# Modulation rows of a two-block transformer: running sums on VectorE and one TensorE product in place of sixteen column-tiled products

## The reference, cut to what matters

```python
lam = exp(sum(lp[0] * lp[1])) - exp(sum(lp[2] * lp[3])) + lam_init
a = softmax(sc, axis=-1)                       # D head: two score maps
attn = a[:, :, 0] - lam * a[:, :, 1]
out = rmsnorm(attn @ v, subln_g) * (1.0 - lam_init)

c_act = silu(c)                                # (1, 2048)
mod = (c_act @ ada_w[l] + ada_b[l])[:, None, :]    # (2048, 12288), 100 MB
sh1, sc1, g1, sh2, sc2, g2 = split(mod, 6, axis=-1)
```

## Time and profile before

| | us |
|---|---|
| median of 3 runs | 2505.77 |
| lowest and highest run | 2504.7 to 2508.65 |
| span of the profiled execution (first to last instruction) | 2501.1 |
| TensorE busy | 2349.9 |
| VectorE, ScalarE, GpSimd busy | 847.8, 855.6, 899.7 |

### The profile page before, as it was taken

One profiled execution on the slowest core, in us unless ns is written; L12 is line 12 of the kernel. 1 busy time (PEld: TensorE's weight loads), 2 busy tenths in 40 slices (PEclk: granted clock), 3 DMA queues, 4 the chain that ended last, 5 costly groups with the idle time before them and its releaser, 6 DMA issues.

```text
span 2501.1 us, 30365 instructions
## 1 busy us (share of the span) xinstructions
PE 2349.9 (94%) x12117; PEld 1533.1 (61%) x12117; DVE 847.8 (34%) x1377; ACT 855.6 (34%) x1583; POOL 899.7 (36%) x395
## 2 busy tenths in 40 slices
PE   7999999999999998999899997999999999999997
PEld 5667777876677787778687776444444444444442
DVE  4132643122335447255443743111122211222213
ACT  4334444443344443453323643111111222111211
POOL 5465655865556567884344362000000000000000
PEclk9999999999999999999999998999999999999999
DMA  8666666576666562441222336999999999999996
GB/s 323 253 269 269 269 260 244 194 311 254 243 262 273 227 263 98 168 169 70 77 92 101 136 121 286 385 428 428 427 428 429 429 428 429 428 429 429 428 428 273
DMA packets 60518, 716.56 MB, mean 286 GB/s; under 512 B 10992, under 2 KB 11600, under 8 KB 17152
## 3 DMA queue, kind: packets, MB, share of 16 engines
q1 hardware_dynamic: 58512, 712.25, 69.6%
q10 hardware_dynamic: 1904, 2.86, 0.3%
HBM read 710.85 MB, written 4.24 MB: 286 GB/s over the span
## 4 chain that ended last, share of the span: by engine, by line
issue 39%; PE 17%; DVE 3%; ACT 1%; DMA 1%; DVEq 0%; POOLq 0%; POOL 0%; ACTq 0%
PE bank L373 5%; PE bank L427 2%; PE bank L383 2%; PE bank L437 1%; PE bank L508 1%; PE bank L514 1%; PE bank L611 1%; DMA weight_ring<-in_w_in_dram 1%; PE bank L512 1%; PE bank L476 0%; PE bank L477 0%; ACT w_hi_parts L2447 0%; PE bank L473 0%; PE bank L466 0%; PE bank L359 0%
## 5 line engine op out<-in xcount | busy, mean ns | idle before, releaser
L2135 POOL TENSOR_TENSOR weight_ring_parts<-weight_ring,w_hi_parts 128x1024 fp32r<-128x1024 f32 (+2 forms) x368 | 872.0, 2392 | 602.6 <-ACT w_hi_parts L2447 601.4
L2447 ACT ACTIVATE w_hi_parts<-weight_ring 128x1024 fp32r<-128x1024 f32 (+2 forms) x368 | 376.4, 1041 | 449.5 <-PE bank L2222 219.2
L1480 POOL TENSOR_TENSOR rms_out<-rms_in,minus_half 128x2 f32<-128x2 f32 x2 | 1.4, 697 | 967.8 <-DVE rms_in L1821 955.8
L1563 PE MATMUL bank<-weight_ring,qk_t 128*64 128x512 f32 x1024 | 224.5, 593 | 12.3 <-DMA weight_ring<-in_expert_w_up_dram 12.3
L2211 PE MATMUL bank<-w_hi_parts,h_t_parts 128*128 128x512 f32 (+1 forms) x768 | 212.9, 401 | 2.0 <-ACT w_hi_parts L2447 2.0
L2211 PE MATMUL bank<-w_hi_parts,x_res_parts 128*128 128x512 f32 (+1 forms) x768 | 198.4, 382 | 0.0
L2222 PE MATMUL bank<-weight_ring_parts,h_t_parts 128*128 128x512 f32 (+1 forms) x768 | 193.3, 380 | 0.0
L1563 PEld LDWEIGHTS bank<-weight_ring,qk_t 128*64 128x64 f32 x1024 | 77.2, 137 | 156.6 <-issue 156.6
L2211 PEld LDWEIGHTS bank<-w_hi_parts,h_t_parts 128*128 128x128 f32 x768 | 132.5, 190 | 48.8 <-issue 18.9
L2211 PEld LDWEIGHTS bank<-w_hi_parts,x_res_parts 128*128 128x128 f32 x768 | 140.5, 189 | 29.6
L2222 PEld LDWEIGHTS bank<-weight_ring_parts,h_t_parts 128*128 128x128 f32 x768 | 139.8, 188 | 28.5
(11 more groups left out here) (465 smaller groups left out, 3570.8 us busy)
## 6 DMA issues: line engine op xcount, KB each, us to landing
weight_ring<-in_w_in_dram SPq DMA_DIRECT2D x64, 2048.0 KB, 8.0
weight_ring<-in_ada_w_dram SPq DMA_DIRECT2D x48, 2048.0 KB, 11.8
weight_ring<-in_expert_w_gate_dram SPq DMA_DIRECT2D x32, 2048.0 KB, 27.0
weight_ring<-in_expert_w_up_dram SPq DMA_DIRECT2D x32, 2048.0 KB, 18.3
weight_ring<-in_expert_w_down_dram SPq DMA_DIRECT2D x32, 2048.0 KB, 24.1
weight_ring<-in_w_out_dram SPq DMA_DIRECT2D x24, 2048.0 KB, 8.7
proj<-in_expert_w_gate_dram SPq DMA_DIRECT2D x16, 2048.0 KB, 26.5
proj<-in_expert_w_down_dram SPq DMA_DIRECT2D x16, 2048.0 KB, 21.9
```

Source lines behind the costliest of these rows:

```text
L1563: last = mm(bank[side][s, :], m.xg[:, 8 * j + k, s], weights(hu + e, 8)[:, k, :], start=j == 0 and k == 0, stop=j == 1 and k == 7)
L2135: nc.gpsimd.tensor_tensor(weights(split, True), weights(split, False), rounded(split).bitcast(f32), ALU.subtract)\
L2447: A_(rounded(split), weights(split, False), ACT.Copy).then_inc(w_hi_ready, 1)
```

## The change

The sixteen products of a modulation row leave TensorE. VectorE forms a running sum over the 16 blocks: each weight block, times its column of `c` (a scalar per partition), plus the sum so far, which stands in a PSUM bank that is free at the time (bank 5 in units 0 to 5, then one of the projection banks); the last one writes the sum to SBUF (`ada_sums`, the space of the repeated column). TensorE folds the 128 partitions with one product, whose weights are one column of -0.5, and `add_row` becomes one instruction that multiplies with -2 and adds the bias. The sums are put between VectorE's tasks by a table: after which step how many of the 16 are to be done; where there is no table, all 16 stand at the unit's start, and "end" is behind the unit's tasks.

In the D heads the first map is no longer scaled by its reciprocal: the second map is weighted with the ratio of the two factors, and the common factor is put into the squares (ScalarE's scale) and into the root.

```diff
+MODS = 16
+MOD_AT = {4: {("mla_rope", 0, 0): 4, "end": 16}, 5: {"begin": 6, ("soft", "M0", 0): 10, ...
+          8: {("diff", "D1", 0): 4, ("soft", "D2", 0): 6, ("soft", "D2", 1): 12, "end": 16},
...
             for s in range(12):
+                ws, mods = [], [(("a", l, s, j), 2 + j, ("ada", l * 24 + 2 * s + j + 1)) for j in (0, 1)]
                 for j in range(1 if s == NARROW else 2):
                     n += 1
-                    keys.append((("w", l, s, j), n % 2, ("piece", ...)))
-                for j in (0, 1):
-                    keys.append((("a", l, s, j), 2 + j, ("ada", l * 24 + 2 * s + j + 1)))
+                    ws.append((("w", l, s, j), n % 2, ("piece", ...)))
+                keys += ws + mods if s == 0 else ws[:1] + mods + ws[1:]
...
         def ada(l, p):
...
-            for j in (0, 1):
...
+            pe.wait_ge(ada_used, 24 * l + 2 * p + 2)
+            nc.tensor.matmul(psTD[0:1, :], half[:, 0:1], ada_sum, start=True, stop=True).then_inc(row_summed, 1)
...
                 link(V.reciprocal(rec[:, :, :], den[:, :, :]))
-                link(V.tensor_scalar(rec[:, 1, :], rec[:, 1, :], lam[:, 1:2], None, ALU.mult))
-                for t in range(TT):
-                    last = V.tensor_scalar(pbuf[:, 0, t, :], pbuf[:, 0, t, :], rec[:, 0, t:t + 1], None, ALU.mult)
-                link(last)
+                link(V.scalar_tensor_tensor(rec[:, 1, :], rec[:, 1, :], lam[:, 1:2], den[:, 0, :], ALU.mult, ALU.mult))
...
                 dve.wait_ge(rms_ready, rr.next())
+                rec = STATS[buffer_of(arg)][5]
+                link(V.tensor_tensor(rec[:, 0, :], rec[:, 0, :], rms[:, 6:8], ALU.mult))
...
+        def mods(l, p, to):
+
+            acc = psO[:, :] if p < 6 else bank[2 * ((sums(p) + 1) % 2)][:, :]
+            while mod_at.k < to:
+                k = mod_at.k
...
+                if k == 0 and p >= 6:
+                    dve.wait_ge(pj_copied, 16 * l + sums(p))
+                if k % 8 == 0:
+                    dve.wait_ge(w_in[2 + k // 8], HALVES.loaded["a", l, p, k // 8])
+                w = ring[:, 2 + k // 8, k % 8 * U:(k % 8 + 1) * U]
+                if k == 0:
+                    ins = V.tensor_scalar(acc, w, ccol[:, k:k + 1], None, ALU.mult)
+                else:
+                    ins = V.scalar_tensor_tensor(acc if k < MODS - 1 else ada_sum, w, ccol[:, k:k + 1], acc, ALU.mult, ALU.add)
...
         def add_row(l, p):
...
-            link(V.tensor_tensor(ada_row[:, :], psTD[0:1, :], ada_b[:, :], ALU.add))
...
+            V.scalar_tensor_tensor(ada_row[:, :], psTD[0:1, :], -2.0, ada_b[:, :], ALU.mult, ALU.add).then_inc(td_copied, 1)
...
+            dve.wait_ge(setup_a, 1)
+            mod_at.k = 0
+            mods(l, 0, MODS)
             if l == 0:
...
                 if early:
                     task(l, p + 1, *early[0])
+                if p:
+                    mods(l, p, MODS)
                 add_row(l, p)
```

More of the change, by code:

```diff
@@ L2252, in ada @@
             if l + p == 0:
-                pe.wait_ge(cb_ready, 1)
+                pe.wait_ge(half_ready, 1)
             pe.wait_ge(td_copied, td.now())
-            for j in (0, 1):
[L2256 to L2262, removed]
+            pe.wait_ge(ada_used, 24 * l + 2 * p + 2)
+            nc.tensor.matmul(psTD[0:1, :], half[:, 0:1], ada_sum, start=True, stop=True).then_inc(row_summed, 1)
             td.next()
@@ L2764, in task @@
                 copy(QK[:, 11:13, :], psTD[:, :])
+                after(l, u, kind, arg, 0)
                 copy(QK[:, 15, :], psTD[:, 0:S])
@@ L2794, in task @@
                     last.then_inc(m_ready, 1)
+                    after(l, u, kind, arg, i)
             elif kind == "diff":
@@ L2813, in task @@
                     g = PROJ[:, t, DG + h * P:DG + (h + 1) * P]
[L2814 removed]
+                    last = V.scalar_tensor_tensor(g, psO[:, t * P:(t + 1) * P], rec[:, 0, t:t + 1], g, ALU.mult, ALU.mult)
                 last.then_inc(o_used, 1)
@@ L2839, in task, with after @@
                     V.tensor_tensor(y_pair(j, "lo"), ps[:, :], y_pair(j, "hi").bitcast(f32), ALU.subtract).then_inc(cop, 1)
+                    after(l, u, kind, arg, i)
+        mod_at = Parts()
+        mod_at.k, mod_at.table = 0, {}
+        def mods(l, p, to):
+            acc = psO[:, :] if p < 6 else bank[2 * ((sums(p) + 1) % 2)][:, :]
+            while mod_at.k < to:
+                k = mod_at.k
+                n = 24 * l + 2 * p
+                if k == 0 and p >= 6:
[7 more added lines that the diff above has]
+                    ins = V.scalar_tensor_tensor(acc if k < MODS - 1 else ada_sum, w, ccol[:, k:k + 1], acc, ALU.mult, ALU.add)
+                if k % 8 == 7:
+                    ins.then_inc(ada_used, 1)
+                    dve.wait_ge(ada_used, n + k // 8 + 1)
+                else:
+                    link(ins)
+                mod_at.k += 1
+        def after(l, p, *at):
+            if p < 12 and at in mod_at.table:
+                mods(l, p, mod_at.table[at])
         def add_row(l, p):
@@ L2924, in _ @@
                     task(l, p + 1, *early[0])
+                if p:
+                    mods(l, p, MODS)
                 add_row(l, p)
+                mod_at.k, mod_at.table = 0, MOD_AT.get(p + 1, {})
                 if p == NARROW - 1:
@@ L2928, in _ @@
                     mla_gains(l)
+                if p + 1 < 12:
+                    mods(l, p + 1, mod_at.table.get("begin", 0) if p + 1 in MOD_AT else MODS)
                 for kind, arg in tasks:
```

29 lines of the change are left out of this document (16 added, 13 removed).

## The result

The changed kernel takes 2567.3 us (median of 4 runs, 2561.0 to 2578.3) against 2505.2 (4 runs, 2500.8 to 2508.7) of the kernel before: a ratio of 1.0252, 95% interval 1.0233 to 1.0271. It is slower by 62 us where 22 us less were forecast, and it lies above the range. The profiled execution has a span of 2576.6 us and a mean granted clock of 0.959 of full (before 2501.1 and 0.982), so its span is 75.5 us longer. It was the slowest of the four, 11 us above their median, so what is read from its trace is compared with 75.5 us and not with 62.

A forecast was written before the change was run, and what follows sets the result against it. TensorE was taken to bound 26 to 930 us. -64.6 - 3.2 + 37.7 + 1.2 (unit 12) + 7.4 = -21.5 on the 2501.1 us span gives 2479.6; the runs' median lies 4.7 higher, so 2484 us, range 2450 to 2506.

The forecast's parts named there:

- What leaves TensorE: Unit ends on TensorE: each of 24 modulation rows falls from 3.57 to 0.88 us, 64.6 us gained.
- Rival 4: The one-column product and its hand-over cost 1.7 us, so 20 us of gain are missing: 2504 us; chance 0.05.
- The other gain: Unit 4, both layers: TensorE's two waits for the copy behind the rotary work go, 3.2 us gained.
- What a sum costs: VectorE: 0.78 us a running sum, 12.5 a row, 300 in all, no GpSimd waits except perhaps the first.
- rival 3: Each running sum waits for GpSimd, a row takes about 12 us more: near 2720 us; chance 0.03.
- Unit by unit: TensorE waits for late sums, mainly in units 4, 7, 8, 9, 10 and layer 1's unit 0: 37.7 us lost.
- The upper end of 2514: Top of the forecast's own case, with waits at 62 us and clock loss at 15; its bottom is 2454.
- The failed step: Second weight half queued behind modulation halves, one ahead in late units, costs nothing; bounds 0 and 1.3 us a late unit.
- The clock: TensorE falls to half clock after long waits: three spells from five chances, 7.4 us lost, bounds 0 and 15.
- Rival 1: VectorE keeps up with the sums, so only unit 12's loss remains: 2439 us; chance 0.15.
- Rival 2: Two-input VectorE instructions in units 7 to 10 wait more for GpSimd, 38 us: 2522 us; chance 0.11.
- I let whatever is gained or lost by then reach the end in full: Behind 930 us nothing is touched, so the gain or loss up to there carries fully to the kernel's end.

The follow-up runs named there:

- run 1: Changed kernel with only one modulation half loaded ahead of the second weight half (w0, a0, w1, a1): 2517.2 us, ratio 1.0049 to the kernel before.
- runs 1 to 3: Run 1, then the changed kernel with 3 of 16 running sums a row: 2543.1 us in its own load order, 2487.9 in run 1's.
- run 5: Kernel before with the change's load order alone (w0, a0, a1, w1), modulation rows on TensorE: 2672.8 us, ratio 1.067.
- run 8: Run 1 plus products that nobody reads, computed while TensorE waits for the sums: 2509.6 us, ratio 1.0015 to the kernel before.

## Why the prediction was wrong, by its own steps

**What leaves TensorE: right.** In the changed kernel the product takes 0.95 us (end of unit 2: 109.56 to the next matmul at 110.51) against 0.88, so the gain is 24 x 2.62 = 63 against 64.6. Rival 4 is out.

```profile
109.56 1.02 PE L2266 MATMUL bank<-ada_sums,minus_half 128*1 128x512 f32 x2
110.51 1.20 PE L2221 MATMUL bank<-w_hi_parts,h_t_parts 128*128 128x512 f32 x4
```

The other gain, 3.2 us of waits behind the rotary work, did not come. In the changed kernel these waits are gone, but TensorE waits for ScalarE in unit 4 instead (1.14 and 1.04 us in layer 0), and the unit is no shorter: 134.52 to 161.9, 27.4 us, against 26.8. In run 1 the rotary waits are 6.1 us (two of 3.0).

**What a sum costs: right.** Of 336 none took over 757 ns, and of the 24 first ones the mean was 750:

```profile
L2869 DVE SCALAR_TENSOR_TENSOR bank<-weight_ring,c_col,bank x336: 741/756/757, 29.8 to 931.0; 128x512 f32<-128x512 f32 x168
```

GpSimd was busy 517 of 904 us in that stretch, so rival 3 is out. The Trainium skill (SBUF — State Buffer, Who interferes with whom) said so of instructions with at most one SBUF input outside the 2-port modes, and the trace agrees: 757 ns at most.

**Unit by unit: right in place and nearly in size.** Unit 4: 3.7 (4.3 forecast), unit 7: 1.5 (1.5), unit 9: 2.6 and 3.1 (2.1), unit 0 of layer 1: 4.7 (4.3), unit 8: 11.2 (8, above its bound of 11). A wait of 0.7 at the end of unit 10 was not forecast. Together 43.9 against 36.1. Inside the units only unit 10's scores were counted, 0.8 us more in each layer; with the late loads they wait 6.5 and 7.3 us more, in run 1 0.2. In run 1, without the late loads, the waits for VectorE inside the units come to some 4 us more than before (L2291 7.6 against 5.8, L2289 2.1), and those for ScalarE's copies to 4.9. The upper end of 2514 was added up wrongly by 2 us (2505.8 - 67.8 + 1.2 + 62 + 15 = 2516), which decides nothing.

**The failed step: "Two halves of 2 MB at the 415 GB/s of the last stage take 10 us, and TensorE reaches that half's first piece 11.8 us in: nothing, bounds 0 and 1.3 us a late unit".** It is worth 50 to 55 us (runs 1 to 3). Three things in it were wrong. First, it took a transfer for its bytes divided by the rate. A half with nothing unfinished ahead of it lands 7.6 to 9.1 us after its issue (mostly near 7.8), where 2 MB at 415 GB/s are 5. In units 8, 9 and 10 exactly one modulation half was ahead, as forecast, and the weight half landed 12.4 to 13.7 us after its issue, not 10. Second, in all but one of the other units two modulation halves were unfinished at its issue, not one, and each is carried in its turn: 11.7 to 14.3 us (unit 7: 13.3). Third, and this is what made the waits, it asked when TensorE needs the piece. In unit 10 the half lands at 366.0, 11.7 us into the unit, which by the prediction's 11.8 would be soon enough for TensorE; yet ScalarE had stood for it for 8.5 us. ScalarE needs it much earlier: it rounds pieces two ahead (240.03 before, 5.4 us into a unit that begins at 234.64), and it takes copies of probabilities, squares and exponentials in the same order. The late load thus reached the softmax of units 6 to 10, by 3 to 8.5 us a wait. What is queued behind a waiting instruction was asked of VectorE and of SP, not of ScalarE.

**The clock: right in kind, too small.** Forecast were three spells and 7.4 us, from five waits. Between 26 and 930 us TensorE had 24 waits of over 1 us, not five of 4, and stood at 1.2 GHz for 109 us before 950 us against 7; what that costs is less than half of it, since TensorE stood still in part of it. In the half-clock stretches it was busy for 72.7 us in all (before 6.2), and half of the difference is 33 us. All five waits that the step had in mind (units 4 and 8 twice, unit 0 of layer 1) were followed by half-clock work, where three were taken: the product behind them took 1.86 us, behind the sums' waits of 3.1 us and less 1.02. Their spells hold 26.6 us of work, so 13.3 us against 7.4. The other spells stand mostly at waits inside the units. Of the 102 us more than before, 41 go with the late loads and so with the failed step; run 1, without them, still has 68 us at half clock.

The terms now add up: -63 for the products, +44 for the sums, +53 inside the units and +33 of clock are 67 for the 69 us measured at the start of the second block.

**Rivals.** Rival 1 is out, since TensorE waited 43.9 us for the sums. Rival 2 named the right side and a wrong mechanism: two-input instructions did grow (L2810 above), but took over waits of instructions that had gone, and the order of loads decides 50 of the 62 us. No rival spoke of the loads. The bound of 1.3 us a late unit hid it, since it was drawn from the same errors. Without them (run 1) the same change gives 2517.2: 33 us above the forecast, outside its range, and slower than before. Of that the product accounts for 2, the sums' waits for 7 (43.6 against 36.1), the rotary waits for 6 (3.2 of gain missed and 2.9 more than before), the other waits inside the units for 7 beyond the 1.6 forecast, and the clock for 12 (TensorE busy for 44.4 us at half clock against 6.2, half of that, less the 7.4 forecast). Together that is 34. So even with the loads in time the forecast was too good by these smaller terms, the clock above all.

**"I let whatever is gained or lost by then reach the end in full": right.** The second block starts 69.1, 13.1 and 170.8 us later than before in the change, run 1 and run 5, and the spans are 75.5, 15.2 and 170.4 longer.

## What to carry to other kernels

A transfer that is issued at the same moment as before still lands later if its queue holds more: count every transfer that is unfinished at its issue, take the time from issue to landing from the trace and not from the rate (here 7.8 us for a lone half, some 5 more for each whole one ahead), and ask for the first engine that touches the data, not the one that computes with it. On an engine that works in order, list what stands behind that first touch. When work moves to an engine with time to spare on average, move it only in the stretches where that engine is idle, and leave the full ones where they were: here 16 of 24 rows moved gave 22 us, and all 24, with nearly the same load order, cost 12 (ratios 0.9910 and 1.0049).

## What the runs showed that was not expected

Neither of these was in the prediction. Products without use in TensorE's waits made the kernel 7.6 us faster (run 8): the half-clock time of the first 950 us fell from 68 to 27 us. And VectorE's small two-input instructions take over the long durations of what stood ahead of them: taking 17.6 us of scalings out of the differences left 36 us where 38 had been.
